# Dense feed-forward of a two-layer decoder trunk: one fp32 matmul per tile in place of three bf16 passes

## What is computed

```python
D_MODEL = 1024; SEQ = 256; D_FF = 2816; N_EXPERTS = 8; D_FF_EXPERT = 3584

def swiglu(h, w_gate, w_up, w_down):
    return (jax.nn.silu(h @ w_gate) * (h @ w_up)) @ w_down

for l in range(2):
    x = x + (g_a * y_a + g_b * y_b + g_c * y_c) @ w_mix_out[l]
    x = x + memory_xattn(rms_norm(x, norm_xattn[l]), mem_n, xa_w_q[l], xa_w_kv[l], xa_w_o[l])
    h = rms_norm(x, norm_ffn[l])
    if l % 2 == 0:
        x = x + swiglu(h, ffn_w_gate[0], ffn_w_up[0], ffn_w_down[0])
    else:
        x = x + moe_swiglu(h, moe_router[0], moe_w_gate[0], moe_w_up[0], moe_w_down[0])
```

## Time and profile before

| | |
|---|---|
| median of 3 runs | 2964.84 us (2962.68 to 2967.07) |
| the profiled execution: its own time | 2964.72 us |
| its span in the trace | 2962.5 us |
| TensorE matmul busy | 2585.5 us (87%), 29799 records |
| TensorE weight loads busy | 2115.7 us (71%) |
| VectorE busy | 1710.2 us (58%) |
| ScalarE busy | 1460.3 us (49%) |
| mean DMA rate over the span | 179 GB/s |
| mean granted TensorE clock | 0.957 |

### The profile page before, as it was taken

The page is one execution under the profiler, slowest core; times in us unless marked ns, Lnnn a source line. Parts: engine busy times, 40 slices in busy tenths (PEclk is TensorE's granted clock), DMA queues, the critical chain, the costliest instruction groups (busy, mean ns, idle before and its releaser), DMA issues.

```text
span 2962.5 us, 67151 instructions
## 1 busy us (share of the span) xinstructions
PE 2585.5 (87%) x29799; PEld 2115.7 (71%) x29818; DVE 1710.2 (58%) x1990; ACT 1460.3 (49%) x1904; POOL 359.0 (12%) x180
## 2 busy tenths in 40 slices
PE   6988898899887989888988999787898898998987
PEld 5866666677565768666666777457888888888886
DVE  2445453244214542445463234128999999999996
ACT  2233334323223431333344232137889889889885
POOL 0000001000000000000001000002334232323232
PEclk9999998999999999999999999998999999999999
DMA  5411021123226634311121133237999999999995
GB/s 178 154 35 58 17 90 40 25 90 118 96 71 214 213 122 125 103 41 31 48 68 37 44 107 101 99 135 272 386 379 391 385 388 385 384 388 385 386 388 200
DMA packets 304032, 531.34 MB, mean 179 GB/s; under 512 B 18528, under 2 KB 145760, under 8 KB 303360
## 3 DMA queue, kind: packets, MB, share of 16 engines
q1 hardware_dynamic: 303600, 525.99, 50.4%
q10 hardware_dynamic: 144, 1.05, 0.1%
HBM read 524.91 MB, written 2.10 MB: 178 GB/s over the span
## 4 chain that ended last, share of the span: by engine, by line
PE 53%; DVE 31%; ACT 8%; issue 6%; DMA 1%; ACTq 0%; DVEq 0%; SPq 0%
DVE arena L2680 22%; PE bank L797 11%; PE bank L698 9%; PE bank L768 4%; PE bank L1268 4%; PE bank L1227 4%; PE bank L763 3%; PE bank L716 2%; DVE yacc L2688 2%; PE bank L1284 2%; PE bank L642 2%; PE bank L1016 1%; PE bank L1368 1%; ACT arena L1874 1%; PE bank L873 1%
## 5 line engine op out<-in xcount | busy, mean ns | idle before, releaser
L2680 DVE TENSOR_TENSOR arena<-ring,arena 128x2048 bf16<-128x2048 f32 x336 | 831.8, 2520 | 5.7 <-ACT arena L1989 5.7
L1989 ACT ACTIVATE arena<-ring 128x2048 bf16<-128x2048 f32 x336 | 639.7, 1910 | 95.6 <-PE bank L1368 24.4
L1368 PE MATMUL bank<-arena 128*128 128x0 bf16 x10752 | 491.3, 209 | 99.9 <-DVE arena L2680 92.2
L1368 PEld LDWEIGHTS bank<-arena 128*128 128x128 bf16 x10752 | 478.2, 100 | 114.7 <-DVE arena L2680 100.6
L797 PE MATMUL bank<-feat,ring 128*128 128x256 f32 x1664 | 434.3, 400 | 8.4 <-ACT ring L1554 2.3
L1518 POOL TENSOR_TENSOR arena<-yacc,arena 128x512 bf16<-128x512 f32 x112 | 301.1, 2700 | 1001.7 <-ACT arena L2012 1001.7
L797 PEld LDWEIGHTS bank<-feat,ring 128*128 128x128 f32 x1664 | 308.6, 196 | 87.1 <-issue 42.9
L1385 PEld LDWEIGHTS bank<-arena 128*128 128x128 bf16 x5376 | 238.1, 98 | 20.6 <-issue 18.4
L1385 PE MATMUL bank<-arena 128*128 128x0 bf16 x5376 | 245.3, 206 | 5.5 <-POOL arena L1518 2.7
L698 PE MATMUL bank<-feat,ring 128*128 128x256 f32 x1056 | 232.7, 384 | 5.6 <-issue 5.6
L698 PEld LDWEIGHTS bank<-feat,ring 128*128 128x128 f32 x1056 | 203.1, 193 | 35.3 <-issue 7.1
(11 more groups left out here) (353 smaller groups left out, 3426.7 us busy)
## 6 DMA issues: line engine op xcount, KB each, us to landing
ring<-in_moe_w_gate SPq DMA_DIRECT2D x112, 1024.0 KB, 8.2
ring<-in_moe_w_up SPq DMA_DIRECT2D x112, 1024.0 KB, 7.8
ring<-in_moe_w_down SPq DMA_DIRECT2D x112, 1024.0 KB, 8.2
ring<-in_w_in SPq DMA_DIRECT2D x76, 1024.0 KB, 5.1
ring<-in_xa_w_kv SPq DMA_DIRECT2D x16, 1024.0 KB, 5.4
ring<-in_ffn_w_gate SPq DMA_DIRECT2D x11, 1024.0 KB, 5.4
ring<-in_ffn_w_up SPq DMA_DIRECT2D x11, 1024.0 KB, 5.5
ring<-in_ffn_w_down SPq DMA_DIRECT2D x11, 1024.0 KB, 6.7
```

Source lines behind the costliest of these rows:

```text
L1368: m = mm(o, w[k // 4][wi][:, k % 4, col:col + P], xg[:, e % 2, xi, k, :].shape_from_register(width[e % 2]), start=i == 0 and k == 0, stop= ...
L1989: sc.activation(w_parts[b][0], ring[:, b * FFN_SLOT:(b + 1) * FFN_SLOT], ACT.Copy).then_inc(S["w_hi"], 1)
L2680: v.tensor_tensor(w_parts[b][1], ring[:, b * FFN_SLOT:(b + 1) * FFN_SLOT], w_parts[b][0], ALU.subtract).then_inc(S["w_lo"], 1)
```

## The change

In layer 0's feed-forward TensorE reads the fp32 chunks in the ring, the fp32 rows `feat` and the fp32 gated values `silu_t` directly, with one matmul in place of three. ScalarE's and VectorE's conversions of weights, rows and gated values go for that layer. A slot is free again when TensorE is past its last matmul on it (`wb_used`), and TensorE waits for the load itself (`slot0` to `slot5`). The slots are taken in another order, 4, 5, 3, 0, 1, 2. At the start of layer 1 SyncE waits for `wb_used` ahead of the first mixer chunk and for `down_full` ahead of the fourth. The experts' counts of chunks are set off by the 33 of the dense layer.

```diff
 FFN_SLOT, FFN_BUFS = 2048, 6
+FFN_ORDER, FFN_CHUNKS = (4, 5, 3, 0, 1, 2), 33
 LEAST = 96
 FE_STEP = 512
 STEPS = FE // FE_STEP
...
@@ -571,9 +572,12 @@
             def ring_free(l, base):
 
                 n = nff[0]
-                b = n % FFN_BUFS
+                b = n % FFN_BUFS if l else FFN_ORDER[n % FFN_BUFS]
                 if n - base >= FFN_BUFS:
-                    sp.wait_ge(S["w_lo"], n - FFN_BUFS + 1)
+                    if l:
+                        sp.wait_ge(S["w_lo"], n - base - FFN_BUFS + 1)
+                    else:
+                        sp.wait_ge(S["wb_used"], n - FFN_BUFS + 1)
                 elif b < MIX_SLOTS:
                     sp.wait_ge(S["weights_used"], sp_s.last[b] + 1)
                 else:
@@ -586,10 +590,11 @@
 
             for l in range(LAYERS):
                 sp_s.phase()
-                if l:
-
-                    sp.wait_ge(S["w_lo"], nff[0])
                 for i, ch in enumerate(mix_chunks(l)):
+                    if l and i == 0:
+                        sp.wait_ge(S["wb_used"], nff[0] - 3)
+                    if l and i == 3:
+                        sp.wait_ge(S["down_full"], 1)
                     if i == MIX_SLOTS:
                         if l:
 
...
 
             def weights_of(*shape):
 
-                b = nff[0] % FFN_BUFS
+                n = nff[0]
                 nff[0] += 1
-                pe.wait_ge(S["w_lo"], c.need("w_lo"))
-                return [view(w_parts[b][i], 0, *shape) for i in range(2)]
+                b = FFN_ORDER[n % FFN_BUFS]
+                pe.wait_ge(S[f"slot{b}"], ffn_due[n])
+                return view(ring, b * FFN_SLOT, *shape)
 
             def ffn(steps):
 
@@ -1263,14 +1269,10 @@
                         if due is not None:
                             pe.wait_ge(S["act_t"], due)
                         for col, w in ((0, wg), (T, wu)):
-                            for n, (wi, xi) in enumerate(PASSES):
-                                for k in range(KT):
-                                    m = mm(bk(b, col, T), w[wi][:, k, j * P:(j + 1) * P], feat_parts[xi][:, k, :],
-                                           start=n == 0 and k == 0, stop=n == 2 and k == KT - 1)
-                                    if n == 0 and k == 0 and not col and bufs_owed[0]:
-
-                                        m.then_inc(S["wb_used"], bufs_owed[0])
-                                        bufs_owed[0] = 0
+                            for k in range(KT):
+                                m = mm(bk(b, col, T), w[:, k, j * P:(j + 1) * P], feat[:, k, :], start=k == 0, stop=k == KT - 1)
+                            if j and not col:
+                                m.then_inc(S["wb_used"], 1)
                         m.then_inc(S["gu_full"], 1)
                     wd = weights_of(2, D)
                     if f == 0:
@@ -1280,20 +1282,15 @@
                         pe.wait_ge(S["act_t"], c.need("act_t"))
                         for t in range(TT):
                             for h in range(2):
-                                for n, (wi, xi) in enumerate(PASSES):
-                                    m = mm(bk(4 + 2 * t + h), act_parts[xi][:, nact[0] % 4, t * P:(t + 1) * P],
-                                           wd[wi][:, j, h * 512:(h + 1) * 512],
-                                           start=f == 0 and j == 0 and n == 0, stop=f == steps - 1 and j == 1 and n == 2)
-                                    if j == 0 and t == 0 and h == 0 and n == 0:
-
-                                        m.then_inc(S["wb_used"], 2)
+                                m = mm(bk(4 + 2 * t + h), silu_t[:, nact[0] % 4, t * P:(t + 1) * P], wd[:, j, h * 512:(h + 1) * 512],
+                                       start=f == 0 and j == 0, stop=f == steps - 1 and j == 1)
+                                if j == 0 and t == 0 and h == 0:
+                                    m.then_inc(S["wb_used"], 1)
                         nact[0] += 1
-                    bufs_owed[0] = 1
-                m.then_inc(S["down_full"], 1)
+                    m.then_inc(S["wb_used" if f < steps - 1 else "down_full"], 1)
                 c.skip("x_new", 4)
 
             nact = [0]
...
             nf = [0]
 
-            nff = [0]
-
-            def high_part():
-
-                n = nff[0]
-                nff[0] += 1
-                b = n % FFN_BUFS
-
-                act.wait_ge(S[f"slot{b}"], ffn_due[n])
-
-                due = c.need("wb_used", 1, spare=FFN_BUFS)
-                if due is not None:
-                    act.wait_ge(S["wb_used"], due)
-                sc.activation(w_parts[b][0], ring[:, b * FFN_SLOT:(b + 1) * FFN_SLOT], ACT.Copy).then_inc(*c.inc("w_hi"))
-
-            def ffn(steps, more=False):
+            nff = [FFN_CHUNKS]
+
+            def ffn(steps):
                 for f in range(steps):
                     for j in range(2):
                         n = nf[0] % 4
                         nf[0] += 1
                         act.wait_ge(S["gu_full"], c.need("gu_full"))
                         sc.activation(silu_t[:, n, :], bk(n, 0, T), ACT.Silu).then_inc(*c.inc("silu"))
...
                 norm(xt, "norm_ffn", l, feat, (3, 1))
-
-                c.skip("feat_half", 8 if l else 12)
-                act.wait_ge(S["feat_half"], c.need("feat_half", 4))
-                act.wait_ge(*c.last())
-                sc.activation(feat_parts[0], feat[:, :, :], ACT.Copy).then_inc(*c.inc("f_hi"))
                 if l == 0:
-                    for _ in range(3):
-                        high_part()
                     ffn(FF // 256)
                 else:
+                    c.skip("feat_half", 24)
+                    act.wait_ge(S["feat_half"], c.need("feat_half", 4))
+                    act.wait_ge(*c.last())
+                    sc.activation(feat_parts[0], feat[:, :, :], ACT.Copy).then_inc(*c.inc("f_hi"))
                     moe()
             act.wait_ge(S["mo_x"], 4 * NE)
...
                 for f in range(steps):
                     for j in range(2):
                         n = nf[0] % 4
                         nf[0] += 1
                         dve.wait_ge(S["silu"], c.need("silu"))
-                        v.tensor_tensor(silu_t[:, n, :], bk(n, T, T), silu_t[:, n, :], ALU.mult).then_inc(*c.inc("act_f"))
-                        dve.wait_ge(*c.last())
-                        v.tensor_copy(act_parts[0][:, n, :], silu_t[:, n, :]).then_inc(*c.inc("act_f"))
-                        dve.wait_ge(*c.last())
-                        v.tensor_tensor(act_parts[1][:, n, :], silu_t[:, n, :], act_parts[0][:, n, :], ALU.subtract
-                                        ).then_inc(*c.inc("act_t"))
-                        if f < steps - 1 or more:
-                            low_part()
-                    if f < steps - 1 or more:
-                        low_part()
+                        v.tensor_tensor(silu_t[:, n, :], bk(n, T, T), silu_t[:, n, :], ALU.mult).then_inc(*c.inc("act_t"))
                 dve.wait_ge(S["down_full"], c.need("down_full"))
                 for t in range(TT):
                     for h in range(2):
                         o = xt[:, t, h * 512:(h + 1) * 512]
-                        if e is None:
-                            v.tensor_tensor(o, bk(4 + 2 * t + h), o, ALU.add).then_inc(*c.inc("x_new"))
-                        else:
-                            v.scalar_tensor_tensor(o, bk(4 + 2 * t + h), gates[:, t, bass.ds(e, 1)], o, ALU.mult, ALU.add
-                                                   ).then_inc(*c.inc("x_new"))
+                        v.tensor_tensor(o, bk(4 + 2 * t + h), o, ALU.add).then_inc(*c.inc("x_new"))
                 dve.wait_ge(*c.last())
 
```

More of the change, by code:

```diff
@@ L98 @@
         "at_L at_max at_exp at_p at_T at_PT at_O at_Of mix_full "
-        "w_hi w_lo wb_used f_hi act_f gu_full silu act_t down_full rt_full rt_d rt_e "
+        "w_hi w_lo wb_used f_hi gu_full silu act_t down_full rt_full rt_d rt_e "
         "mo_xT mo_tok mo_m mo_A mo_yb mo_g0 mo_xg mo_used mo_act mo_tr mo_ah mo_al "
@@ L1282, in ffn @@
                             for h in range(2):
-                                for n, (wi, xi) in enumerate(PASSES):
-                                    m = mm(bk(4 + 2 * t + h), act_parts[xi][:, nact[0] % 4, t * P:(t + 1) * P],
-                                           wd[wi][:, j, h * 512:(h + 1) * 512],
-                                           start=f == 0 and j == 0 and n == 0, stop=f == steps - 1 and j == 1 and n == 2)
-                                    if j == 0 and t == 0 and h == 0 and n == 0:
-                                        m.then_inc(S["wb_used"], 2)
+                                m = mm(bk(4 + 2 * t + h), silu_t[:, nact[0] % 4, t * P:(t + 1) * P], wd[:, j, h * 512:(h + 1) * 512],
+                                       start=f == 0 and j == 0, stop=f == steps - 1 and j == 1)
+                                if j == 0 and t == 0 and h == 0:
```

(15 more changed lines are left out.)

## The result

The changed kernel takes 3010.55 us (median of 4 runs, 3009.12 to 3012.64) against 2964.82 us (4 runs). The ratio is 1.0155, 95% interval 1.0142 to 1.0168: slower by 46 us. The prediction was 3009.6 us.

What follows compares the result with a forecast made beforehand. TensorE was taken to bound the dense feed-forward, with conversions on the path only ahead of its first matmul. Steps +55.8, start -8.8 and clock -2.1 gave +44.9 on 2964.7: 3009.6 us, range 3003 to 3018.

Steps and rivals of the forecast that it cites:

- The price of a matmul: Dense feed-forward: a fp32 matmul costs 0.432 us (256 columns) or 0.858 (512); eleven steps of 20.73, not 15.66: +55.8 us.
- the 0.05 us between gate and down: Each dense feed-forward step: the 0.05 us between the gate and up stretch and the down stretch stays.
- The rival of two streams: Dense feed-forward: a fp32 matmul costs two bf16 streams, not four; steps of 10.39 us, 2895.8 us in all, faster; 4%.
- The start: Ahead of the first feed-forward matmul: conversions go, TensorE waits for the rows only, starting at 909.61, not 918.42: -8.8 us.
- The clock: First gate and up stretch: runs at the full 2.4 GHz instead of starting at the 1.2 GHz level: -2.1 us.
- The gated values: Ahead of down's second half: product done some 0.9 us after gate and up, covered by 3.4 us of down: no cost.
- the ring: Dense feed-forward weight slots: freed only after TensorE's use, but loads need 152 GB/s against 311 moved: no cost.
- the hand-over: Into the next layer: three chunks wait for the step before last, the fourth for the last down: no cost.
- The rival of a feed that binds: Dense feed-forward loads: transfers below 152 GB/s lengthen steps; a tenth slower, nine steps gain 2 us each: 3028 us; 1%.
- The expectation on the forms of the trace: Feed-forward trace: 704 records on gate and up, about 176 on down, 22 activations, 22 products, transfers at about 152 GB/s.
- the clock at stage starts: Sums, norm and projections after the feed-forward: unchanged, but their start at low clock may shift up to 2.1 us either way.

Runs made afterwards that it cites:

- the last run above: Kernel before with only gate and up of the first dense feed-forward step in fp32, the rest in bf16 parts: 2955.91 us, ratio 0.9966.
- three runs: Against the kernel before: the whole change, 3010.55 us; only gate and up in fp32, 2986.64 us; only down in fp32, 2983.35 us.
- the two runs on the start: Kernel before with only the change's slot order: 2968.94 us, ratio 1.0009; changed kernel with slots in order 0 to 5: 3014.50 us, ratio 1.0168.

## Why the prediction was right, point by point

- **The price of a matmul.** This step carried the sign: two records per fp32 matmul, each as long as two bf16 passes. Forecast 0.432 and 0.858 us, 20.73 a step, +55.8 in all. Measured 20.68, 11 x (20.68 - 15.66) = +55.2. The difference is the 0.05 us between gate and down, which I took for a gap that stays. It is none: the trace of the kernel before lacks one of the 24 records of each down stretch (253 records, but 264 weight loads), and where all are there the stretch takes 5.18 us with no idle time ahead of it, behind bf16 (929.25 + 10.48 to 939.73 in the last run above) as behind fp32. So 24 passes take 5.18 us, 0.216 each; I had divided 5.13. The step before stays 15.66 us. The rival of two streams falls with three runs and with the half of the inputs left out: its 2895.8, 2914.6 and 2946.1 us against 3010.55, 2986.64 and 2983.35.
- **The start.** Forecast -8.8; measured by the windows -8.85. The first matmul comes 0.11 us behind VectorE's last row (907.15 + 2.04 to 909.30), 0.10 forecast. It is the conversions and the loads together, as the two runs on the start show. SyncE's order was read rightly: both chunks are issued at 853.3 and 853.9 us.
- **The clock.** Forecast -2.1. The first stretch takes 14.05, 0.24 over the later ones, where it was 2.06 over: -1.8. The sum of steps, start and clock is 44.5 us, 44.9 forecast.
- **Costs put at nothing.** The gated values, the ring and the hand-over cost nothing. No idle time stands ahead of a down matmul, three slots do as well as six, and layer 1 starts 13.61 us behind the sums, 13.62 before. The rival of a feed that binds falls with the ring.
- **The expectation on the forms of the trace.** 704 and 176 records, 22 activations and 22 products, and 148 GB/s for 152 were found.
- **What was too small.** I gave the clock at stage starts up to 2.1 us outside the feed-forward. The query projection of layer 1 alone took 3.06 us more (see below), and the experts 1.83 less, though nothing in them was changed. Neither is in the forecast. That the whole time comes out within 1 us of it (3009.6 against 3010.55) is in part luck: these two partly cancel.

## What to carry to other kernels

Price a fp32 matmul by the distance between those who read its results, and count the program's instructions against the trace's records before dividing a group's busy time by its count: here the quotient is half the price, and the sign of the change hangs on it. Where TensorE is the bound and the other engines have room, three bf16 passes beat one fp32 matmul by a quarter (0.328 against 0.432 us); work taken off engines that are off the path pays only where it stood on it, at the start. There the dearer form can be used for just the first pieces, while the cheaper one is being prepared.

## What the runs showed of the hardware

The low clock after one and the same gap does not last equally long in all kernels. Ahead of layer 1's query projection TensorE stands idle for 4.39 us, transposes, and stands idle for 1.40 in both kernels, yet the projection took 27.86 us in one profile and 30.92 in the other:

```profile
1909.47 27.86 PE L698 MATMUL bank<-feat,ring 128*128 128x256 f32 x128 [1.40 <-issue]
```
```profile
1953.56 30.92 PE L703 MATMUL bank<-feat,ring 128*128 128x256 f32 x128 [1.40 <-issue]
```

In both the granted clock falls to 0.50, the 1.2 GHz level, within 1 us of the start of the transposes. In the kernel before it is back ahead of the projection; in the changed one it stays low until about 6 us into it. A window of the kernel before, then two of the changed one:

```profile
1910.00:1912.00 2.00, 2.00 (x11) 1.77 (x10) 0.00 (x0) 0.00 (x0) 0.00 (x0) 1.00 0.00 0
```
```profile
1951.00:1955.00 4.00, 2.60 (x10) 1.96 (x9) 1.93 (x4) 0.68 (x2) 0.00 (x0) 0.50 0.67 233
1955.00:1960.00 5.00, 5.00 (x14) 3.99 (x13) 0.00 (x0) 0.00 (x0) 0.00 (x0) 0.52 0.00 0
```

Of the ten profiles of this case five have 27.86 us at this place, four 30.92 or 30.93, and one (half of the inputs) 29.24. The changed kernel, the only one with two profiles, has 30.92 and 30.93, so whether it differs between executions of one kernel is not shown, and what decides it was not tried. Either way 3 us at one such gap, in code that nobody changed, is no evidence on a change. A stage measured between two of its own marks in the trace repeated to 0.01 us (240.99, 240.99, 241.00), while the device times of the same three executions were 3009.92, 3013.62 and 3017.45.
